# Expert biases of a mixture-of-experts stage summed once per expert into banks of their own and copied by ScalarE into each unit's product banks

## What is computed

```python
gu = lax.ragged_dot(xs, w_gu, group_sizes) + b_gu[e_sorted]
g, u = gu[:, :EXPERT_FF], gu[:, EXPERT_FF:]
g = jnp.minimum(g, SWIGLU_LIMIT)
u = jnp.clip(u, -SWIGLU_LIMIT, SWIGLU_LIMIT)
act = (u + 1) * (g * jax.nn.sigmoid(SWIGLU_ALPHA * g))
out = lax.ragged_dot(act, w_down, group_sizes) + b_down[e_sorted]
out = out * gate_w.reshape(-1)[order][:, None].astype(out.dtype)
y = jax.ops.segment_sum(out, src, num_segments=n_tok)
```

## Time and profile before

| | us |
|---|---|
| median of 3 runs | 2640.77 |
| lowest, highest | 2635.83, 2645.7 |
| the profiled execution | 2641.59 |
| its span, first to last instruction | 2639.9 |
| PE busy in the span | 2405.0 (91%) |
| DVE busy | 1545.6 (59%) |
| ACT busy | 1337.7 (51%) |
| POOL busy | 835.9 (32%) |

### The profile page before, as it was taken

One profiled execution on the slowest core, in us unless ns is written; L12 is line 12 of the kernel. 1 busy time (PEld: TensorE's weight loads), 2 busy tenths in 40 slices (PEclk: granted clock), 3 DMA queues, 4 the chain that ended last, 5 costly groups with the idle time before them and its releaser, 6 DMA issues.

```text
span 2639.9 us, 55169 instructions
## 1 busy us (share of the span) xinstructions
PE 2405.0 (91%) x19141; PEld 1347.5 (51%) x19142; DVE 1545.6 (59%) x1828; ACT 1337.7 (51%) x1395; POOL 835.9 (32%) x945
## 2 busy tenths in 40 slices
PE   6999988899989949899899998889988999999991
PEld 3555544667755535455455554445544555545550
DVE  2222246566635665961953768999679715165975
ACT  1111144356532244862843658888678624165861
POOL 1212222410003354343332443434334423233422
PEclk9999989899999969999999999999999999999996
DMA  8000043430032285982964779999989925177974
GB/s 331 11 18 18 9 153 123 125 90 0 0 114 89 96 290 167 388 300 69 361 230 136 263 262 334 397 397 393 332 306 398 331 57 194 28 256 274 356 281 182
DMA packets 180248, 538.48 MB, mean 204 GB/s; under 512 B 20672, under 2 KB 37490, under 8 KB 180142
## 3 DMA queue, kind: packets, MB, share of 16 engines
q1 hardware_dynamic: 150620, 487.79, 48.7%
q0 software_dynamic: 26656, 46.85, 7.9%
q10 hardware_dynamic: 2916, 3.14, 0.4%
HBM read 493.11 MB, written 45.20 MB: 204 GB/s over the span
## 4 chain that ended last, share of the span: by engine, by line
PE 46%; DVE 6%; issue 6%; ACT 2%; DMA 2%; POOL 1%; ACTq 0%; DVEq 0%; POOLq 0%; SPq 0%
PE psum L2054 42%; DVE arena L1825 5%; PE psum L2043 2%; PE psum L2038 2%; PE psum L2032 1%; ACT arena L1647 1%; DMA arena<-in_w_down 1%; DVE arena L1919 0%; DVE arena L1884 0%; DVE arena L1920 0%; DMA expert_lists<-arena 0%; POOL expert_lists L1502 0%; DVE arena L1933 0%; ACT arena L1695 0%; DVE arena L1874 0%
## 5 line engine op out<-in xcount | busy, mean ns | idle before, releaser
L2054 PE MATMUL psum<-arena 128*64 128x512 bf16 x12528 | 1419.0, 382 | 72.2 <-DVE arena L1874 39.4
L2054 PEld LDWEIGHTS psum<-arena 128*64 128x64 bf16 x12528 | 714.3, 111 | 727.1 <-DVE arena L1825 53.7
L1825 DVE TENSOR_TENSOR arena<-arena 128x2048 bf16<-128x2048 f32 x384 | 862.8, 2287 | 184.5 <-ACT arena L1647 184.2
L1647 ACT ACTIVATE arena<-arena 128x2048 bf16<-128x2048 f32 x384 | 723.0, 1904 | 99.0 <-DVE arena L1825 70.0
L1557 POOL DMA_INDIRECT expert_sums<-arena x90 | 186.9, 2076 | 670.7 <-issue 648.2
L551 PE MATMUL psum<-arena 128*128 128x512 f32 (+2 forms) x864 | 298.9, 504 | 1.1 <-ACT arena L407 1.1
L551 PEld LDWEIGHTS psum<-arena 128*128 128x128 f32 x864 | 150.8, 190 | 133.8 <-issue 129.1
L1874 DVE TENSOR_TENSOR arena<-psum,arena 128x512 bf16<-128x512 f32 x87 | 59.9, 688 | 233.6 <-ACT arena L1689 233.6
L1528 POOL DMA_INDIRECT arena<-expert_inputs,arena x88 | 107.5, 1222 | 202.5 <-PE psum L2032 176.9
L1685 ACT ACTIVATE arena<-psum 128x1024 bf16<-128x1024 bf16 x87 | 88.6, 1018 | 154.8 <-issue 152.8
L1700 ACT ACTIVATE arena<-psum,arena 128x512 f32<-128x512 f32 x87 | 59.3, 682 | 202.1 <-PE psum L2054 202.1
(11 more groups left out here) (269 smaller groups left out, 2186.8 us busy)
## 6 DMA issues: line engine op xcount, KB each, us to landing
arena<-in_w_gu SPq DMA_DIRECT2D x256, 1024.0 KB, 16.0
arena<-in_w_down SPq DMA_DIRECT2D x128, 1024.0 KB, 13.8
arena<-in_w_ada SPq DMA_DIRECT2D x12, 2048.0 KB, 9.6
arena<-in_x_sample SPq DMA_DIRECT2D x16, 512.0 KB, 3.4
arena<-in_w_in SPq DMA_DIRECT2D x3, 2048.0 KB, 20.3
expert_sums<-arena SPq DMA_DIRECT2D x10, 512.0 KB, 6.4
expert_inputs<-arena SPq DMA_DIRECT2D x10, 512.0 KB, 2.8
x_after_mixing<-arena SPq DMA_DIRECT2D x9, 512.0 KB, 2.7
```

What stands on the lines that cost most here:

```text
L1647: nc.scalar.activation(high(e, p, c), raw[p][c], ACT.Copy).then_inc(sem(f"hi_made{c}"), 1)
L1825: nc.vector.tensor_tensor(w_lo[p][c], raw[p][c], high(e, p, c), ALU.subtract).then_inc(sem(f"lo_made{c}"), 1)
L2054: last = nc.tensor.matmul(bank(b)[group(g)], parts[part][:, cols], w[:, kk, g * H:(g + 1) * H], start=False, stop=(k == KT - 1 and part == 1))
```

## The change

Three PSUM banks more are used: `T_GATE`, `T_UP` and `T_Y`. In an expert's first unit PE sums the gate bias into `B_GATE` and `T_GATE` and the up bias into `B_UP` and `T_UP`, and the down bias into `T_Y` (in the very first unit also into `B_Y`). In other units PE sums no bias. ACT copies the T banks into the product banks for every unit: `lay_y_up` (two copies) at the start of a unit's body, ahead of `act_hi` and of a last unit's `hi`; `lay_gate` behind the `hi` that follow `keep_x`, ahead of `result`. PE's matmuls onto the banks wait for these copies (`gate_laid`, `up_laid`, `y_laid`) in every unit, the first too. Both bias-row DMAs for the next expert are issued in an expert's first unit, behind `result`.

```diff
+                def lay_y_up(j):
+                    act.wait_ge(sem("y_made"), j + (DELAY - 1))
+                    wait(act, sem("act_made"), j)
+                    nc.scalar.activation(bank(B_Y), bank(T_Y), ACT.Copy).then_inc(sem("y_laid"), 1)
+                    nc.scalar.activation(bank(B_UP), bank(T_UP), ACT.Copy).then_inc(sem("up_laid"), 1)
+
+                def lay_gate(j):
+                    wait(act, sem("g_made"), j)
+                    nc.scalar.activation(bank(B_GATE), bank(T_GATE), ACT.Copy).then_inc(sem("gate_laid"), 1)
...
+                    if not opening(j):
+                        lay_y_up(j)
                     if last:
                         divide(2 if first else 1)
                     if not opening(j):
                         act_hi(j - 1)
                     sigmoid(j)
-                    if last:
-                        wait(act, sem("used4"), n)
-                        bias_gu(e + 1)
                     divide(2)
...
                     divide(2 if first else 1)
-                    if not opening(j):
+                    lay_gate(j + 1)
+                    if opening(j):
+                        act.wait_ge(sem("y_bias_made"), 1)
+                    else:
                         result(j - 1)
-                        if first:
-                            bias_dn(e)
+                    if first and not final(e):
+                        wait(act, sem("used4"), j + 1)
+                        bias_gu(e + 1)
+                        bias_dn(e + 1)
                     divide(None)
...
-                def down(j, p, e1):
-                    wait(pe, sem("b_dn_in"), e1 * 16)
-                    wait(pe, sem("y_made"), j + DELAY)
-                    bias(B_Y, rows_dn, 0)
+                def down(j, p, e1, entering=None):
+                    wait(pe, sem("y_laid"), j + 1)
+                    if entering is not None:
+                        wait(pe, sem("b_dn_in"), entering * 16 + 16)
+                        bias(T_Y, rows_dn, 0)
...
-                    wait(pe, sem("b_gu_in"), e * 16 + 16)
                     if not opening(j):
-                        wait(pe, sem("g_made"), j)
-                    bias(B_GATE, rows_gu, 0)
+                        wait(pe, sem("gate_laid"), j)
+                    if first:
+                        wait(pe, sem("b_gu_in"), e * 16 + 16)
+                        bias(B_GATE, rows_gu, 0)
+                        bias(T_GATE, rows_gu, 0)
...
-                        wait(pe, sem("act_made"), j)
-                    bias(B_UP, rows_gu, 2)
+                        wait(pe, sem("up_laid"), j)
+                    if first:
+                        bias(B_UP, rows_gu, 2)
+                        bias(T_UP, rows_gu, 2)
```

## The result

The changed kernel takes **2777.0 us** (median of 4 runs, 2775.1 to 2781.7) against 2641.5 before (median of 4): a ratio of 1.0511, with a 95% interval of 1.0490 to 1.0532. It is slower, as forecast, but by 136 us instead of 50, and outside the range of 2655 to 2715.

The account below looks back on a forecast made before the run. PE's expert products were taken as the bound. Saved pairs -20.5, first units +26 and +0.3, very first unit +4.1, single-unit experts +40, tail +0.3 gave +50 us: 2691 us, 1.9% slower, range 2655 to 2715.

Parts of the forecast that it names:

- The count of pairs and their price: PE's bias matmul pairs: 261 become 161, so 100 pairs at 0.216 us, 21.6 us, leave PE.
- The two waits of a first unit: Experts with more units: PE waits 0.3 us for the up copy, 1.4 for the gate copy; 15 x 1.75 = 26 us.
- The price of a copy: Each ACT copy of a bank takes 0.5 us in a chain and 0.6 us to its end.
- the DMA of the rows: Single-unit expert's next bias rows land near T + 20.3, costing nothing while the up copy comes at T + 33.
- The three units around a single-unit expert: Single-unit expert and two units behind: 63.96 us grows by 5.0, 1.2 of it slow clock; 40 us for eight.
- The very first unit: PE's second gate block waits for the gate copy behind two `hi`: 4.1 us later.
- The end: Tail of the stage: two copies ahead of the last `act_hi`, less a pair, add 0.3 us.
- the other units: Units away from single-unit experts hold 95 of the 100 saved pairs, giving -20.5 us.
- A: Rival: all copies finish before PE needs them, so only the pairs count: 2619 us; chance 0.04.
- B: Rival: single-unit experts' loss is hidden under DVE, so the 40 us goes: about 2651 us; chance 0.10.
- C: Rival: a copy costs 1.02 us as `keep_x` does, 38 us more: 2729 us; chance 0.06.
- D: Rival: the bias-row DMA decides at single-unit experts, landing after T + 32, each us beyond costing 8; chance 0.03.

Follow-up runs that it names:

- experiment 1: Changed kernel with ACT's expert loop moved by 80 instructions by satisfied waits run once ahead of it, loop unchanged: 2701.2 us, ratio 1.0223.
- experiment 6: Changed kernel with the next expert's gate and up bias-row DMA issued behind `sigmoid` and two `hi` instead of behind `result`: 2781.1 us, ratio 1.0522.
- experiments 3 and 4: Changed kernel with ACT's expert loop moved by 128 and by 256 instructions by satisfied waits run once ahead of it: 2777.4 and 2786.9 us.
- experiment 2: Kernel before with ACT's loop grown from 274 to 320 instructions by satisfied waits, no copies, biases as before: 2717.1 us, ratio 1.0282.
- experiments 9 to 11: Changed kernel, loop moved by 80, copies and row DMA issued earlier; then two `hi` ahead of copies; then single-unit row DMA earlier still: 2653.8, 2646.6, 2646.4 us.
- experiment 8: Changed kernel with the next unit's down and up copies right behind `result` and ACT's loop moved by 80 instructions: 2712.1 us, ratio 1.0252.

## Why the prediction was wrong, by its own steps

**What was right.** Without the fetch gaps (experiment 1) the changed kernel takes 2701 us against the 2691 predicted, inside the range; part of that closeness is luck, as the terms below show. The count of pairs and their price hold (middle units 16.69 us, a unit ahead of a first one 17.13). The two waits of a first unit were put at 0.3 and 1.4 us and are 0.26 and 1.59: such a unit takes 19.46 us, where the 17.34 + 1.75 of the sum gives 19.1. The price of a copy, 0.5 in a chain and 0.6 to its end, was right from the read of a bank into SBUF. The trace gives 0.58 us for a write to PSUM beside 0.60 for a read of the same size into SBUF. The Trainium skill ("ScalarE: Activation LUTs", section "Step-by-step: what each stage is for") calls PSUM the lower-latency port for an ACTIVATE's destination; here that is 0.02 us at most. That the DMA of the rows costs nothing while the up copy is late was said with a landing time 0.4 us off, and experiment 6 bears it out.

**The step that failed: an edit's code was taken to be free.** The sum priced the copies by what they do on ACT and had no term for their length. The order printed ahead showed the bodies growing, and the trace of before had a row for instruction packets, 26 on queue 14, that I did not read. The loop grew from 274 to 320 instructions and, by the table of experiments 3 and 4, now touches a fourth block; 14 gaps of 4.0 to 7.6 us follow. Experiment 1 puts them at 76 us with the clock time that they cause; experiment 2 shows them without the change, at 74 with its added waits. None of the rivals had this mechanism, so the range was too narrow for a reason outside it.

**Mis-sized terms.** The three units around a single-unit expert were put at 69.0 us. Without fetch gaps the first takes 71.7 (29.6, 24.9, 17.1), 2.7 us more. The blocks behind idle times are slow there twice, 6.87 and 7.40 us instead of 5.35, where I had added 1.2 us for one. The very first unit was put 4.1 us later; its T came at 996.7 in experiment 1 instead of 992.6, which is that. With the loop unmoved it is 1000.4, of which 3 us came before: PE's transposes ahead of that block start at 986.4 instead of 983.4.

Over the stage of experiment 1's profiled execution, term by term: the eight single-unit experts with the units behind cost 45 us, not 40. The 15 first units cost 31, not 26: 2.05 us a unit instead of 1.75. The end costs 4.6, not 0.3: the last product block starts 1.2 us later behind `turn_act` and takes 8.19 us instead of 5.37. Against these, the other units saved 24.6 us, not 20.5. They hold 107 pairs fewer and not 95: the sum took 5 of the 100 saved pairs to lie at single-unit experts, whose units in truth hold 5 more than before (the up block behind the wait was given no pair, and has two). So the growth of 60 us for the 50 predicted is 14 us by which waits and blocks were put too low, less 4 us by which the saving was.

**The rivals.** A, hidden copies, would need all three places mended, and even then reaches the level of before (experiments 9 to 11), not 2619. B fails: experiments 1 and 6 leave the single-unit experts' loss in place. C fails by the copy's 0.58 us. D is in the trace with 60 us of waits and is worth nothing by experiment 6, as it was priced.

## What to carry to other kernels

When an edit adds instructions to a loop with run-time bounds, count the loop's instructions on that engine and look at the page's instruction packets before and after: if they grow with the turns of the loop, move or shorten the loop before judging the edit. If an instruction's stop is put down to nothing but issue, look whether it stands where a loop jumps back. Work that is moved to an engine with idle time costs what is queued ahead of it at the moment of need, and what is queued behind it; both are read from one unit's timeline, as the gate copy's 1.6 us here. The largest wait in a table may be worth nothing when a later wait holds the same path, so undo one at a time.

## What the runs showed of the hardware that was not expected

ACT's loop of 320 instructions ran without instruction fetches at one place (start 671) and with some 5 packets of 8,192 bytes for each jump back at three others (591, 719, 847). The cost was a stop of 4.0 to 7.6 us at each jump, nearly 3% of this kernel. A wait of 2.06 us instead of 1.59 ahead of a product block went with a block of 7.06 us instead of 5.37, with the granted clock at 0.76 instead of 1.00 (experiment 8 beside experiment 1). A copy of one bank from PSUM to PSUM by ACT took 0.58 us, hardly less than a copy into SBUF (0.60).
